# Rotary step without its TensorE products; compression products ahead of the tokens' products

## The reference

```python
half = ROPE_DIM // 2                                  # 8
x1, x2, xp = x[..., :half], x[..., half:ROPE_DIM], x[..., ROPE_DIM:]
rope(x) = concatenate([x1 * c - x2 * s, x1 * s + x2 * c, xp])   # 16 of a head's 64 values

qn     = rmsnorm(heads(nq), qnorm_g)                  # 8 heads of 64
q_rope = rope(qn)
kc = rmsnorm(silu(blocks(kcm) @ w1_k) @ w2_k, ...)    # compression: 15 blocks of 32 tokens
vc = silu(blocks(vcm) @ w1_v) @ w2_v
p_cmp = masked_softmax(qn @ kc.T * scale)             # without the rotary step
k_sl, k_wn = rope(rmsnorm(ksl)), rope(rmsnorm(kwn))   # 2 heads each
o_slc, o_win = attention(q_rope, k_sl, vsl), attention(q_rope, k_wn, vwn)
h = h + concatenate([y_hg, gated(o_cmp, o_slc, o_win)]) @ w_out
```

## Time and profile before

| | |
|---|---|
| runs | 988.89, 989.20, 989.45 us, median 989.2 us |
| profiled execution: own time, span | 991.16 us, 989.5 us |
| TensorE busy (matmuls), weight loads | 968.3 us (98%), 880.5 us |
| VectorE, ScalarE, GpSimd busy | 754.5, 617.7, 6.9 us |
| mean granted TensorE clock | 1.000 |

### The profile page before, as it was taken

The page is one execution under the profiler, slowest core; times in us unless marked ns, Lnnn a source line. Parts: engine busy times, 40 slices in busy tenths (PEclk is TensorE's granted clock), DMA queues, the critical chain, the costliest instruction groups (busy, mean ns, idle before and its releaser), DMA issues.

```text
span 989.5 us, 18815 instructions
## 1 busy us (share of the span) xinstructions
PE 968.3 (98%) x7642; PEld 880.5 (89%) x7642; DVE 754.5 (76%) x1132; ACT 617.7 (62%) x918; POOL 6.9 (1%) x17
## 2 busy tenths in 40 slices
PE   6999999999999999999999999999999999999997
PEld 6998888998978889989998999999988988888886
DVE  7968676787676786797778776868977698768675
ACT  5745785676437775778467655556666576555564
POOL 2000000000000000000000000000000000000000
PEclk9999999999999999999999999999999999999999
DMA  9665513365637131835655656556473456655541
GB/s 304 200 167 171 171 60 112 123 218 172 174 118 229 44 124 53 272 117 182 202 170 174 210 172 202 178 187 203 120 235 99 148 168 198 191 195 184 178 161 43
DMA packets 143357, 164.00 MB, mean 166 GB/s; under 512 B 6302, under 2 KB 129832, under 8 KB 143288
## 3 DMA queue, kind: packets, MB, share of 16 engines
q1 hardware_dynamic: 142408, 161.97, 51.1%
q10 hardware_dynamic: 464, 0.93, 0.3%
q0 software_dynamic: 416, 0.12, 0.1%
HBM read 161.95 MB, written 1.05 MB: 165 GB/s over the span
## 4 chain that ended last, share of the span: by engine, by line
PE 79%; DVE 10%; ACT 4%; DMA 3%; issue 2%; SPq 0%; DVEq 0%; ACTq 0%
PE ps L483 16%; PE ps L484 16%; PE ps L485 16%; PE ps L1263 14%; PE ps L1261 7%; DVE panels_low L2005 3%; DMA panels<-in_w_in 2%; ACT panels_high L1377 2%; DVE squares L1968 1%; PE ps L501 1%; PE ps L688 1%; DVE input_parts L1964 1%; PE ps L713 1%; DMA panels<-in_w_pg 1%; PE ps L784 1%
## 5 line engine op out<-in xcount | busy, mean ns | idle before, releaser
L2005 DVE TENSOR_TENSOR panels_low<-panels,panels_high 128x2048 fp32r<-128x2048 f32 (+1 forms) x145 | 327.5, 2262 | 80.0 <-ACT panels_high L1377 79.8
L1377 ACT CAST panels_high<-panels 128x2048 fp32r<-128x2048 f32 (+1 forms) x145 | 273.1, 1886 | 101.4 <-PE ps L485 64.0
L483 PE MATMUL ps<-input_parts,panels_low 128*128 128x256 f32 x832 | 241.6, 290 | 2.2 <-DVE panels_low L2005 1.5
L484 PE MATMUL ps<-input_parts,panels_high 128*128 128x256 f32 x832 | 235.2, 283 | 0.0
L485 PE MATMUL ps<-input_parts,panels_high 128*128 128x256 f32 x832 | 235.1, 283 | 0.0
L1263 PE MATMUL ps<-input_parts,panels_high 128*128 128x512 f32 x608 | 214.0, 395 | 0.0
L1261 PE MATMUL ps<-input_parts,panels_low 128*128 128x256 f32 x608 | 170.6, 281 | 0.7 <-DVE panels_low L2005 0.7
L483 PEld LDWEIGHTS ps<-input_parts,panels_low 128*128 128x128 f32 x832 | 159.1, 191 | 7.4 <-issue 3.9
L484 PEld LDWEIGHTS ps<-input_parts,panels_high 128*128 128x128 f32 x832 | 159.2, 191 | 0.7 <-issue 0.5
L485 PEld LDWEIGHTS ps<-input_parts,panels_high 128*128 128x128 f32 x832 | 159.2, 191 | 0.0
L1263 PEld LDWEIGHTS ps<-input_parts,panels_high 128*128 128x128 f32 x608 | 114.1, 188 | 26.4
(11 more groups left out here) (342 smaller groups left out, 1620.8 us busy)
## 6 DMA issues: line engine op xcount, KB each, us to landing
panels<-in_ffn_up SPq DMA_DIRECT2D x44, 1024.0 KB, 5.1
panels<-in_w_in SPq DMA_DIRECT2D x29, 1024.0 KB, 5.5
panels<-in_ffn_down SPq DMA_DIRECT2D x22, 1024.0 KB, 4.8
panels<-in_mix_w_in SPq DMA_DIRECT2D x20, 1024.0 KB, 5.5
panels<-in_w_out SPq DMA_DIRECT2D x8, 1024.0 KB, 5.0
panels<-in_w_pg SPq DMA_DIRECT2D x8, 1024.0 KB, 5.1
panels<-in_mix_w_out SPq DMA_DIRECT2D x8, 1024.0 KB, 5.2
panels<-in_w_in SPq DMA_DIRECT2D x6, 512.0 KB, 5.7
```

The costliest lines, as they stand in the source:

```text
L483: pe.matmul(dst, w[1], x[0], start=start, stop=False if not kw else True, **kw)
L484: pe.matmul(dst, w[0], x[1], start=False, stop=False if not kw else True, **kw)
L1377: nc.scalar.copy(high_slots[slot][:, 0:size], raw[n % SLOTS][:, 0:size]).then_inc(high_ready, 1)
L2005: V.tensor_tensor(low_slots[slot][:, 0:size], raw[n % SLOTS][:, 0:size], high_slots[slot][:, 0:size].bitcast(F32), ALU.subtract).then_inc( ...
```

## The change

The rotary step leaves TensorE. VectorE writes the cosine product into `QR` itself and the sine product, now with the sign in the table, into `UW`. GpSimd then issues four DMAs for q (8 partitions of 1024 columns each) and four for k (8 partitions of 512), which add the sine rows onto the rows eight partitions away. The 12 matmuls of lines 858, 859, 867 and 868 and ScalarE's two copies to `QR` go, in all of both layers. "k_pad" waits for k's four DMAs and reads SBUF; it stands after "o_square". TensorE waits for q's DMAs and for `kz` before the masks. The product `hid4` stands ahead of the tokens' products; "q_norm" and "k_norm" stand after level 6; `hid` follows at once, and both halves of hgo0 stand after it. The splits move too: hgo1's right after "q_norm" on VectorE, hz0's right after "hidden".

```diff
...
     for h in (0, 8, 64, 72):
         cos[h:h + 8] = np.cos(ang.astype(np.float32))
-        sin[h:h + 8] = np.sin(ang.astype(np.float32))
+        sin[h:h + 8] = np.sin(ang.astype(np.float32)) * (-1 if h % 64 else 1)
...
@@ -817,19 +813,6 @@
                     two_chunks(name, b, (key, l))
                     some(2)
                     todo(step)
-                tokens([f"vv{n}_{l}" for n in range(NT)], 5, [(f"vv{h}", l) for h in range(2)], VV,
-                       lambda: some(2))
-                todo(("gates",))
-
-                pe.wait_ge(qsq_ready, l + 1)
-                for j in range(2):
-                    product(f"qss{j}_{l}", 1 + j, 512, head_ones, SQ[:, j * 512:(j + 1) * 512])
-                todo(("q_norm",))
-                pe.wait_ge(ksq_ready, l + 1)
-                product(f"kss_{l}", 4, 512, head_ones, UK[:, 0:512])
-                todo(("k_norm",))
-                some(2)
-
                 pe.wait_ge(blocks_ready, l + 1)
                 begin(f"hid4_{l}", 3)
                 for kv in range(2):
@@ -843,7 +826,18 @@
                 release(("cmp0", l))
                 release(("cmp1", l))
                 todo(("hidden_parts",))
-                gate_chunk()
+                tokens([f"vv{n}_{l}" for n in range(NT)], 5, [(f"vv{h}", l) for h in range(2)], VV,
+                       lambda: some(2))
+                todo(("gates",))
+
+                pe.wait_ge(qsq_ready, l + 1)
+                for j in range(2):
+                    product(f"qss{j}_{l}", 1 + j, 512, head_ones, SQ[:, j * 512:(j + 1) * 512])
+                pe.wait_ge(ksq_ready, l + 1)
+                product(f"kss_{l}", 4, 512, head_ones, UK[:, 0:512])
+                some(2)
+                todo(("q_norm",))
+                todo(("k_norm",))
                 drained(pe, f"hid4_{l}")
                 begin(f"hid_{l}", 3)
                 for kv in range(2):
@@ -851,22 +845,11 @@
                                     const("sum_of_four"), start=True, stop=True)
                 done(f"hid_{l}", ins)
                 todo(("hidden",))
-
-                pe.wait_ge(rope_ready, l + 1)
-                for j in range(2):
-                    begin(f"qr{j}_{l}", 1 + j)
-                    pe.matmul(ps[1 + j][:, :], ident, UW[:, j * 512:(j + 1) * 512], start=True, stop=False)
-                    done(f"qr{j}_{l}", pe.matmul(ps[1 + j][:, :], const("rot"),
-                                                 UW[:, 1024 + j * 512:1024 + (j + 1) * 512],
-                                                 start=False, stop=True))
-                    todo(("copy", f"qr{j}"))
+                gate_chunk()
+
+
                 some(2)
                 gate_chunk()
-                pe.wait_ge(k_rope_ready, l + 1)
-                begin(f"kr_{l}", 4)
-                pe.matmul(ps[4][:, :], ident, UK[:, 0:512], start=True, stop=False)
-                done(f"kr_{l}", pe.matmul(ps[4][:, :], const("rot"), UK[:, 512:1024], start=False, stop=True))
-                todo(("k_pad",))
                 pe.wait_ge(w2_landed, 48 * (l + 1))
                 pe.wait_ge(hidden_ready, l + 1)
                 product(f"kc_{l}", 5, 32, W2[:, 0:P], HID[:, 0:32])
@@ -903,6 +886,7 @@
                                         start=False, stop=True)
                     done(f"o{g}_{l}", ins)
                 todo(("o_square",))
+                todo(("k_pad",))
                 gate_chunk()
 
                 pe.wait_ge(kc_ready, l + 1)
@@ -920,8 +904,8 @@
                     product(f"oss{g}_{l}", 5 + g, 512, ones, SQ[:, g * 512:(g + 1) * 512])
                 todo(("o_norm",))
                 gate_chunk()
-                drained(pe, f"qr1_{l}")
-                drained(pe, f"kr_{l}")
+                pe.wait_ge(q_turned, 64 * (l + 1))
+                pe.wait_ge(kz_ready, l + 1)
                 for n in range(NT):
                     drained(pe, f"vv{n}_{l}")
                 pe.wait_ge(gates_ready, l + 1)
...
@@ -1607,6 +1590,7 @@
                         head_rinv([f"qss{j}_{l}" for j in range(2)], HZ[:, :], 64, 1024).then_inc(q_rinv_ready, 1)
                     elif step == "k_norm":
                         head_rinv([f"kss_{l}"], UK[:, 512:1024], 64, 512).then_inc(k_rinv_ready, 1)
+                        split_high(place, SPLIT_NO[("hgo1", l)] + 1)
                     elif step == "hidden_parts":
                         copy_out(f"hid4_{l}", HP, bank(f"hid4_{l}")[:, 0:256])
                     elif step == "hidden":
@@ -1614,14 +1598,13 @@
                         f(SS[:, 0:64], bank(f"hid_{l}")[:, 0:64], ACT.Exp, scale=-1.0).then_inc(hid_exp_ready, 1)
                     elif step == "k_pad":
 
-                        name = f"kr_{l}"
-                        full(act, name)
-                        src = v3(bank(name), 2)
+                        act.wait_ge(k_turned, 64 * (l + 1))
+                        src = UK[:, 0:512].rearrange("p (k t) -> p k t", k=2)
                         for g in range(2):
                             s = src[64 * g:64 * g + 64]
                             nc.scalar.copy(kz[0:64, :, 0, g, :], s)
                             ins = nc.scalar.copy(kz[64:128, :, 1, g, :], s)
-                        ins.then_inc(free(name), 1)
+                        ins.then_inc(kz_ready, 1)
                     elif step == "spread":
                         act.wait_ge(level_ready, 16 * l + 2 * NBLK_LVL)
                         for c in range(NBLK):
@@ -1643,7 +1626,7 @@
                     elif step == "kc_norm":
                         head_rinv([f"kcss_{l}"], SS[:, 64:96], 64, 32).then_inc(kc_rinv_ready, 1)
                     elif step == "o_norm":
-                        act.wait_ge(rope_ready, l + 1)
+                        act.wait_ge(kz_ready, l + 1)
                         head_rinv([f"oss{g}_{l}" for g in range(2)], UK[:, :], P, 1024).then_inc(o_rinv_ready, 1)
                     elif step == "cmp_softmax":
                         act.wait_ge(cmp_shift_ready, l + 1)
@@ -1667,7 +1650,7 @@
                         mixed_high(l, [f"on{g}_{l}" for g in range(2)], (3,))
 
                     in_units = (in_units or step == "scores") and step != "on"
-                    parts_out = (parts_out or step == "hidden_parts") and (step, *arg) != ("copy", "qr1")
+                    parts_out = (parts_out or step == "hidden_parts") and step != "hidden"
                     kv_in = kv_in or step == "cmp_kv"
                     if not parts_out and (not in_units or step == "turned" and arg[0] % 2 == 1):
                         split_high(place, len(SPLIT_KEYS) if kv_in else SPLIT_NO[("hz1", l)])
@@ -2315,11 +2298,11 @@
                         dve.wait_ge(q_rinv_ready, l + 1)
                         link(V.scalar_tensor_tensor(QN[:, :], QN[:, :], GQ[:, l:l + 1], HZ[:, :],
                                                     ALU.mult, ALU.mult))
-                        qn4 = v3(QN, 4)
-                        for i, tab in enumerate(("cos", "sin")):
-                            ins = V.tensor_tensor(UW[:, i * 1024:(i + 1) * 1024].rearrange("p (j t) -> p j t", j=4),
-                                                  qn4, const(tab).unsqueeze(1).to_broadcast([P, 4, T]), ALU.mult)
+                        for tab, terms in (("cos", QR[:, :]), ("sin", UW[:, 1024:2048])):
+                            ins = V.tensor_tensor(v3(terms, 4), v3(QN, 4),
+                                                  const(tab).unsqueeze(1).to_broadcast([P, 4, T]), ALU.mult)
                         ins.then_inc(rope_ready, 1)
+                        split_low(place, SPLIT_NO[("hgo1", l)] + 1)
                     elif kind == "k_norm":
                         dve.wait_ge(k_rinv_ready, l + 1)
                         for j in range(2):
@@ -2419,7 +2402,7 @@
                         V.scalar_tensor_tensor(Y[:, 1536:2048], bank(name)[:, :], 0.5, NZ[:, 512:1024],
                                                ALU.mult, ALU.mult).then_inc(free(name), 1)
                         mixed_low(l, 3)
-                    parts_out = (parts_out or kind == "hidden_parts") and kind != "cmp_kv"
+                    parts_out = (parts_out or kind == "hidden_parts") and kind != "hidden"
                     in_units = (in_units or kind == "scores") and kind != "on"
                     if (kind, *arg) == ("copy", "hgo0"):
                         split_low(place, SPLIT_NO[("hgo1", l)] + 1)
@@ -2756,6 +2739,16 @@
             for tile, r, n, c0, c1, src in vec_dmas[0::2]:
                 pool.dma_start(vrows[r:r + n, tile, c0:c1], src).then_inc(pool_vec_landed, 16)
 
+            half_rows = [(h + a, h + 8 - a) for h in (0, 64) for a in (0, 8)]
+
+            for l in range(DEPTH):
+                pool.wait_ge(rope_ready, l + 1)
+                for src, dst in half_rows:
+                    pool.dma_start(QR[dst:dst + 8, :], UW[src:src + 8, 1024:2048], accum_op=ALU.add).then_inc(q_turned, 16)
+                pool.wait_ge(k_rope_ready, l + 1)
```

(14 more changed lines are left out.)

## The result

The changed kernel takes **995.59 us** (median of 4 runs, 995.39 to 995.85) against 989.33 of the kernel before (4 runs, 988.89 to 989.60): 1.0064 times as long, 95% interval 1.0046 to 1.0081, so 6.3 us slower. The forecast was 991.8, with 986.8 to 997.2 as its range. The profiled execution took 995.39 us, its span is 993.4 and the mean granted clock 0.992, where it was 1.000.

The account below looks back on a forecast made before the run. TensorE, busy 98% of the span, bounds the kernel. New waits on VectorE's queue outweigh the matmuls removed: 1.9 + 0.6 = 2.5 to 2.6 us more than the median of 989.2, so 991.8 us, range 986.8 to 997.2.

Parts of the forecast that it names:

- the clock's rival: TensorE falls to its lower clock in the new waits: 994.4 us in one layer (0.13), 997.0 in both (0.18).
- Removed: q's and k's rotary matmuls leave TensorE: 3.6 and 1.7 us, 5.3 us in a layer, 10.6 in both.
- The queue on VectorE: From level 6 at 87.75, closed queue: `hidden_ready` at 99.7, bank 0 free at 103.3; error perhaps 0.5 us.
- The waits: TensorE newly waits 4.3 us before kc for `hidden_ready`, then 3.2 us before hgo1 for bank 0.
- The stage: First tokens' or hid4 product to recurrence's output: 34.8 us in both layers, 1.9 and 0.6 us lost.
- The term that failed: TensorE's clock in the two new waits: the forecast's sum added nothing for a fall.
- the rival with a chance of 0.18: TensorE's clock falls in the new waits of both layers: 997.0 us (995.2 to 998.6).
- the forecast's own case: Both new waits in each layer without a clock price: 991.8 us, spanning 990.5 to 993; chance 0.42.
- The base: The profiled execution took 991.16 us, the runs' median 989.2, 2 us lower; the forecast was set against the median.
- GpSimd: Its adding DMAs cost nothing, landing at 5.4 us; rival: landings of 16 us, 4 us per layer, 1000 us, 0.04.
- one split less: Rival: hz0's low part doesn't hold up level 7, bank 0 free at 101.1: 987.4 us, chance 0.15.
- Faster, in full: Rival: nothing new is waited for, 10.6 us of matmuls and 1.2 of old waits go: 977.4 us, chance 0.05.

Follow-up runs that it names:

- g1_first_on_tensor: f5_hidden_first with the rotary step back on TensorE, q's products behind `cross` and k's behind the next gate chunk: 986.92 us.
- f5_hidden_first: The changed kernel with VectorE's and ScalarE's queues in TensorE's order, hidden, hgo1's split and level 7 ahead of q's and k's norms and rotary terms: 977.24 us.
- e3_bank_one: The changed kernel with gate panel hgo1 in bank 1, so that it doesn't wait for VectorE's copy of level 7: 990.93 us.
- e4_split_late: The changed kernel with hz0's low part behind level 7 on VectorE, not between hidden and level 7: 991.83 us.
- e2_fill_first: The changed kernel with only the first new wait filled, by four unread products of constants ahead of kc's product: 994.96 us.
- f6_rotary_alone: The kernel before with the rotary step alone changed (VectorE's terms, GpSimd's adds), hid4 and hid in their old places: 988.90 us.

## Why the prediction was right and where it was off

- **The number:** the kernel got slower, as forecast with 0.68, and 995.59 lies in the range of 986.8 to 997.2. It doesn't lie in the forecast's own range of 990.5 to 993: the extra time was forecast as 2.5 us and measured as 6.3. The range held it because it was drawn wide enough for the clock's rival.
- **Removed:** 5.3 us a layer were right; with nothing waiting, g1_first_on_tensor less f5_hidden_first shows 5.1 in the stage and 9.7 in the time for both.
- **The queue on VectorE:** forecast from level 6 at 87.75 to `hidden_ready` at 99.7 and bank 0 at 103.3. In the trace 88.00, 100.06 and 103.59 (the ends of the two copies), later by 0.25, 0.36 and 0.3 us; a quarter of a microsecond of each is the later start of level 6.
- **The waits:** 4.3 and 3.2 forecast. The first is 4.31. The second is recorded as 2.47, from the slower vc's end; hgo1 stands at 103.64 against 103.35.
- **The stage:** 34.8 forecast, 36.3 and 36.2 measured, and 34.84 and 34.86 with the waits filled. The sum was right but for one term.
- **The term that failed** is the clock's, which the forecast's own sum put at nothing: the granted clock was to stay at 1.00 through both waits. It fell at the end of the first wait in both layers and cost 1.5 us each (4.46 and 4.40 against 2.95), 3 of the 3.8 us by which the time lies above 991.8. That was the rival with a chance of 0.18, at 997.0 (995.2 to 998.6), and the time is at its lower end, since its price, 1.7 to 3.4 a layer from the start of the kernel, was set too high for this place; in e3_bank_one's second layer 2.3 were seen. The rule of the Trainium skill (TensorE: Matmul & The Clock Gate, What's actually happening), that an idle TensorE is throttled, agrees with the trace: a granted clock of 0.50 from 101 to 107, behind 4.31 us without a product.
- **What was weighed wrongly:** the end of the kernel showed that a standstill of 5 us brings the clock down, and the two waits of 4.3 and 3.2 us with 0.37 of work between were called open. A standstill of 7.9 us with a speck of work in it was nearer to the row of 5 us than to the waits under 2 us at which the clock had stayed, so the fall in both layers deserved more than the 0.42 of the forecast's own case.
- **The base:** the profiled execution of before has 678.1 us behind its second output product (span less 311.42), the changed one 676.4, and f5_hidden_first 676.4 too. So the profiled execution was about 1.7 us longer in a part that the change doesn't touch, and setting the sum against the median was right. Of 6.3 us, 5.5 lie in the two stages (3.5 and 2.0) and 0.3 around the span (1.7 before, 2.0 after); about 0.4 isn't located.
- **GpSimd:** nothing forecast, 0.5 us in the medians, not shown to be theirs. The landings, 4.6 and 3.3 us, were under the 5.4 of the earlier trace rows, and an issue took 0.8 instead of 0.53 (12.9 us more of GpSimd's time for 16 issues). The trap named from the Trainium skill (SBUF — State Buffer, "DVE blocks DMA") would make them later; no run here shows TensorE held up by one. In f5_hidden_first k's landings took 6.3 us and ScalarE waited for the last; by what they were slower, no run tells.
- **Rivals:** "one split less" did not happen, but e4_split_late made it happen: 991.8, and not 987.4, mostly because the clock falls all the same (hgo1's half took 5.29 and 4.31 us for 2.95). "Faster, in full" (977.4) was said to need VectorE 7 us earlier, "for which I see no reason". What the forecast missed is that the order on VectorE could be changed: f5_hidden_first has `cmp_hidden_rep` 8.0 us earlier (91.86 for 99.83) and took 977.24.

## What to carry to other kernels

Taking work off the busiest engine pays only as far as the next engine's results are there when it now asks: put its queue in the order of the asking first, and then the saving pays (here -12 us instead of +6). Before you say that a result can't come sooner, list what stands ahead of it and when each of these is wanted; what nobody wants for 10 us goes behind. Where a wait of some microseconds on TensorE can't be avoided, count the fall of its clock with it; work without use in the wait was cheaper here than the wait left empty (987.32 against 990.93 us).

## What was unexpected of the hardware

- In every run that had a standstill of 4.3 us the clock fell near its end: mostly right at it, in e3_bank_one's second layer about 0.5 us before it, and in e4_split_late's second layer about 0.9 us behind it, when TensorE was at work again. It fell also in a wait of 2.85 us that had only 0.9 us of standstill and a few small products ahead of it (e2_fill_first). A fall cost 1.2 to 2.3 us where hgo1's half stood behind it: that half took between 4.15 and 5.29 us where 2.95 is its time at full clock. The low clock lasted about 3.4 us at some falls and 6.8 at others (e3_bank_one has one of each).
- In f6_rotary_alone the clock came down while TensorE was already busy again: the window 96 to 97 has 1.00 us of work and a clock of 0.55, behind waits of 3.04 and 0.80 us. A wait's price can thus appear in rows behind it.
- An accumulating DMA of GpSimd from SBUF to SBUF, 8 rows of 4 KB or 2 KB, took 0.8 us to issue and 4.6 or 3.3 us to land beside a VectorE without a pause; in f5_hidden_first, where k's followed q's without a gap, 3.0 and 6.3 us.
